# Prompt delta rule: the 16x16 diagonal blocks of the triangular inverse are solved on VectorE instead of four doubling levels on TensorE; the experts' low parts all on VectorE

## The reference

```
A = jnp.where(strict, jnp.einsum('nbhid,nbhjd->nbhij', kb, k) * decay, 0.0)
L = A + jnp.eye(C, dtype=A.dtype)
sol = lax.linalg.triangular_solve(L, rhs, left_side=True, lower=True, unit_diagonal=True)
```

## Time and profile before

| what | value |
|---|---|
| median of 3 runs | 3206.22 us (3206.04 to 3209.23) |
| the profiled execution | 3210.79 us, span 3209.2 us |
| PE busy | 2627.7 us (82%) |
| DVE busy | 1601.7 us (50%) |
| ACT, POOL busy | 1064.6 us (33%), 698.9 us (22%) |
| granted TensorE clock, mean | 0.903 of full |

### The profile page before, as it was taken

How to read it: one execution, slowest core, us unless ns; L and a number is a source line. 1 busy time by engine, 2 the same in 40 slices (tenths; PEclk the granted TensorE clock), 3 DMA queues, 4 the chain that set the end, 5 groups by cost and what they waited for, 6 DMA issues and landing times. The chain is left out here.

```text
span 3209.2 us, 36850 instructions
## 1 busy us (share of the span) xinstructions
PE 2627.7 (82%) x13079; PEld 1953.9 (61%) x13080; DVE 1601.7 (50%) x1864; ACT 1064.6 (33%) x1565; POOL 698.9 (22%) x559
## 2 busy tenths in 40 slices
PE   5799999999998666789987998969648888888840
PEld 2477777777777543644447998945336666666620
DVE  2245445444545321124444456423458888888815
ACT  3123323323332100023333423312136566656602
POOL 1033133123213020011221000000043343344212
PEclk8999999999999767589998999989779999999975
DMA  7300000000000123021106444552369999999625
GB/s 289 133 7 27 20 7 27 27 0 27 27 1 1 45 61 139 1 79 40 39 0 221 140 129 126 149 165 82 119 223 349 334 342 338 337 337 341 236 105 176
DMA packets 252401, 420.95 MB, mean 131 GB/s; under 512 B 30563, under 2 KB 202099, under 8 KB 224228
## 3 DMA queue, kind: packets, MB, share of 16 engines
q1 hardware_dynamic: 228172, 355.72, 32.6%
q0 software_dynamic: 11168, 39.12, 3.4%
q10 hardware_dynamic: 13000, 25.30, 2.1%
HBM read 375.48 MB, written 46.65 MB: 132 GB/s over the span
## 5 line engine op out<-in xcount | busy, mean ns | idle before, releaser
L2356 DVE TENSOR_TENSOR ex_w_r<-ex_w,ex_wh 128x2048 fp32r<-128x2048 f32 x160 | 457.3, 2875 | 110.6 <-ACT ex_wh L2297 110.6
L2297 ACT ACTIVATE ex_wh<-ex_w 128x2048 fp32r<-128x2048 f32 x192 | 360.2, 1912 | 236.8 <-DVE ex_y L2374 98.0
L777 PE MATMUL gd_ps<-hT,gd_w 128*128 128x352 f32 x768 | 245.5, 468 | 13.7 <-DMA gd_w<-in_w_in_dram 8.2
L1716 PE MATMUL mg_psum<-mg_xl,mg_wh 128*128 128x352 f32 x768 | 252.2, 328 | 0.0
L2221 POOL TENSOR_TENSOR ex_w_r<-ex_w,ex_wh 128x2048 fp32r<-128x2048 f32 x32 | 160.2, 5009 | 409.4 <-ACT ex_wh L2297 409.4
L777 PEld LDWEIGHTS gd_ps<-hT,gd_w 128*128 128x128 f32 x768 | 144.0, 195 | 87.0 <-DMA gd_w<-in_w_in_dram 10.0
L1776 DVE TENSOR_TENSOR mg_w_r<-mg_w,mg_wh 128x1024 fp32r<-128x1024 f32 x96 | 129.1, 1349 | 126.7 <-ACT mg_wh L1729 126.6
L542 POOL TENSOR_TENSOR gd_am<-gd_AT,levels 128x512 f32<-128x512 f32 x112 | 143.7, 1300 | 182.8 <-DVE gd_AT L710 96.5
L615 ACT ACTIVATE gd_T<-gd_x 128x512 f32<-128x512 f32 x96 | 57.3, 597 | 325.8 <-PE gd_x L797 325.8
L1729 ACT ACTIVATE mg_wh<-mg_w 128x1024 fp32r<-128x1024 f32 x96 | 101.4, 1056 | 189.5 <-DVE mg_out L1803 126.3
L1888 PE MATMUL op_mix<-op_w,op_mT 128*128 128x512 f32 x288 | 131.0, 615 | 25.5 <-DMA op_w<-in_w_out_dram 25.5
(11 more groups left out here) (571 smaller groups left out, 5689.0 us busy)
## 6 DMA issues: line engine op xcount, KB each, us to landing
ex_w<-in_w_gate_dram SPq DMA_DIRECT2D x64, 1024.0 KB, 7.6
ex_w<-in_w_up_dram SPq DMA_DIRECT2D x64, 1024.0 KB, 7.3
ex_w<-in_w_down_dram SPq DMA_DIRECT2D x64, 1024.0 KB, 6.4
ada_w<-in_w_ada_dram SPq DMA_DIRECT2D x24, 1024.0 KB, 14.5
mg_w<-in_w_in_dram SPq DMA_DIRECT2D x48, 512.0 KB, 3.7
gd_w<-in_w_in_dram SPq DMA_DIRECT2D x32, 512.0 KB, 4.5
expert_out_scratch<-ex_y ACTq DMA_DIRECT2D x32, 512.0 KB, 8.0
mg_w<-in_w_br_gdn_dram SPq DMA_DIRECT2D x24, 512.0 KB, 3.6
```

The lines of the kernel that those rows point to most:

```text
L777: last = nc.tensor.matmul(dst, w[t][:, n, :], c.hT[:, n, at], start=(n == 0), stop=(n == KD - 1))
L1716: last = nc.tensor.matmul(pm[b][q][:, 0:R], a, x, start=(m == 0 and v == 0), stop=(m == KD - 1 and v == 2))
L2297: nc.scalar.activation(wh[at][:], wl[b][u][:], ACT.Copy).then_inc(w_high, 1)
L2356: nc.vector.tensor_tensor(wl_r[b][u][:], wl[b][u][:], wh[at][:].bitcast(F32), ALU.subtract).then_inc(low_v, 1)
```

## The change

In `delta_prompt`, levels 0 to 3 go. In their place AT is stored to a scratch tensor in device memory, SP loads all 64 diagonal 16x16 blocks of the head's eight tiles, one block to a partition (`gd_Ab`, 64x256), and DVE inverts them by forward substitution: 15 columns, each a product (`gd_Tb`) and a subtraction in `gd_Yb`, each waiting for the one before. Y and its transpose go back to scratch tensors whose other entries were zeroed once at the start, and are loaded as full tiles into `gd_Y` and `gd_YT`. Levels 4 and 5 run as before; level 6 uses the 64-row halves of the tiles that are not zero. PE now does four projection units (8 halves) ahead of level 4, none inside level 4, and two units inside levels 5 and 6. V's SiLU on DVE stands behind the whole substitution, and PE's turn of v waits for it.

In `experts`, all six low parts are DVE's, ACT alone copies y (1024 columns), POOL keeps the gathers. w_down is loaded as rows k*128+p (`kmajor`), in pieces of 4 KB instead of 8 KB, and the hidden activation is written without a stride.

```diff
+                    for g in range(2):
+                        sp.wait_ge(ats, i * 8 + g * 4 + 4)
+                        sp.dma_start(image(c.at_s, g), v4(AT[g][:])).then_inc(at_out, 16)
+                    sp.wait_ge(at_out, i * 32 + 32)
+                    sp.dma_start(Ab[:], diagonal(c.at_s)).then_inc(blocks_in, 16)
+                    sp.wait_ge(solved, i + 1)
+                    sp.dma_start(diagonal(c.y_s), Yb[:]).then_inc(y_out, 16)
+                    sp.dma_start(diagonal(c.yt_s), YbT[:]).then_inc(y_out, 16)
+                    sp.wait_ge(y_out, i * 32 + 32)
+                    for g in range(2):
+                        sp.dma_start(v4(Y[g][:]), image(c.y_s, g)).then_inc(y_in[g], 16)
+                        sp.dma_start(v4(YT[g][:]), image(c.yt_s, g)).then_inc(y_in[g], 16)
...
+                    dve.wait_ge(y_out, i * 32)
+                    step(nc.vector.tensor_copy(Yb[:], Ib[:]), 0)
+                    dve.wait_ge(blocks_in, i * 16 + 16)
+                    for j in range(BS - 1):
+                        n, m = BS - 1 - j, j + 1
+                        tmp = Tb[:, 0:n * m].rearrange("p (a b) -> p a b", b=m)
+                        step(nc.vector.tensor_tensor(tmp, Ab[:, j, m:BS].unsqueeze(2).to_broadcast([64, n, m]), Yb[:, j:j + 1, 0:m].to_broadcast([64, n, m]), ALU.mult), 2 * j + 1)
+                        step(nc.vector.tensor_tensor(Yb[:, m:BS, 0:m], Yb[:, m:BS, 0:m], tmp, ALU.subtract), 2 * j + 2)
+                    step(nc.vector.tensor_copy(YbT[:], Yb[:].rearrange("p r q -> p q r")), STEPS - 1)
...
-                def low_last(e, b):
-                    pool.wait_ge(w_high, e * UNITS + 10 if not (isinstance(e, int) and e == NE - 1) else 6 * NE)
-                    nc.gpsimd.tensor_tensor(wl_r[b][5][:], wl[b][5][:], wh[down_slot(b, 1)][:].bitcast(F32), ALU.subtract).then_inc(low_p, 1)
...
-                    nc.scalar.activation(y[b][:, 0:512], pd[:, 0:512], ACT.Copy).then_inc(y_act, 1)
-                    act.wait_ge(y_act, e + 1)
-                    act.wait_ge(y_dve, e + 1)
+                    nc.scalar.activation(y[b][:], pd[:], ACT.Copy).then_inc(copied, 1)
+                    act.wait_ge(copied, e + 1)
...
+                    if not is_first(e):
+                        down_low(e + -1, 1 - b, 1)
```

More of the change, by code:

```diff
@@ L436, in delta_prompt @@
     C4 = 4 * P
+    BS = 16
+    NQ = P // BS
+    STEPS = 2 * BS
+    HP = P // 2
+    IMAGE = NQ * (BS * P + BS)
     C3 = TA // 3
@@ new lines, in body @@
+                    pe.wait_ge(v_silu, i + 1)
+                    pe.wait_ge(capped, i * 8 + 8)
+                    for g in range(2):
+                        turn(pp[g], y[2], g).then_inc(vturned, 1)
+                    if nxt:
+                        for half in range(2):
+                            project(1, 0, half, i + 1)
+                    for l in (4, 5, 6):
+                        for g in range(2):
+                            if l == 4:
+                                pe.wait_ge(kts, i * 2 + g + 1)
+                                pe.wait_ge(y_in[g], i * 32 + 32)
+                            else:
+                                pe.wait_ge(ys, i * 4 + (l - 5) * 2 + g + 1)
+                            if l < 6:
+                                pe.wait_ge(lvl, i * 4 + (l - 4) * 2 + g + 1)
+                                quad(X[g][0], am[g][l % 2], Y[g]).then_inc(p1, 1)
+                            else:
+                                for n in range(4):
+                                    lo, hi = slice(n * P, n * P + HP), slice(n * P + HP, (n + 1) * P)
+                                    last = nc.tensor.matmul(X[g][0][:, lo], AT[g][0:HP, n * P:(n + 1) * P], Y[g][0:HP, lo], start=True, stop=True)
+                                last.then_inc(p1, 1)
+                            if l == 5:
@@ L875, in body @@
                             else:
-                                quad(X[g][1], T1[g], YT[g]).then_inc(p3, 1)
-                        if nxt:
-                            project((l - 1) // 3, (l - 1) % 3, 1, i + 1)
+                                for n in range(4):
+                                    lo, hi = slice(n * P, n * P + HP), slice(n * P + HP, (n + 1) * P)
+                                    last = nc.tensor.matmul(X[g][1][:, hi], T1[g][HP:P, n * P:(n + 1) * P], YT[g][HP:P, hi], start=True, stop=True)
+                                last.then_inc(p3, 1)
+                        if nxt and l > 4:
+                            project(1, l - 4, 1, i + 1)
                     for g in range(2):
-                        pe.wait_ge(yts, i * 12 + 10 + g + 1)
+                        pe.wait_ge(yts, i * 6 + 4 + g + 1)
                         pe.wait_ge(k2s, i * 4 + g * 2 + 2)
@@ L2177, in before, with last_down @@
             return n if is_first(e) else e * UNITS + (n - 2)
+        def last_down(e, half):
+            return 6 * NE - 2 + half if isinstance(e, int) and e == NE - 1 else e * UNITS + (8 + half)
         def up_slot(e, b, u):
@@ L2251, in down @@
                 def down(e, b, half):
-                    if half:
-                        pe.wait_ge(low_p, e + 1)
-                    else:
-                        pe.wait_ge(low_v, e * (UNITS - 1) + 9 if not (isinstance(e, int) and e == NE - 1) else 5 * NE)
+                    pe.wait_ge(w_low, last_down(e, half) + 1)
                     h = wh[down_slot(b, half)]
@@ L2302, in down_high @@
                 def down_high(e, b, n, h):
-                    high(e, b, n, 4 + h, down_slot(b, h), e * UNITS + (8 + h) if not (isinstance(e, int) and e == NE - 1) else 6 * NE - 2 + h)
+                    high(e, b, n, 4 + h, down_slot(b, h), last_down(e, h))
                 def x_high(e):
@@ L2386, in body @@
                     else:
[L2387 removed]
+                        for h in range(2):
+                            down_low(e, b, h)
                     dve.wait_ge(twos, e + 1)
                     dve.wait_ge(used, before(e, 4))
[L2390 to L2391 removed]
+                    nc.vector.tensor_tensor(gu[:], two[:], pu[:], ALU.mult).then_inc(prods, 1)
                     if nxt:
@@ L2395, in body @@
                         up_low(e + 1, 1 - b, 2)
-                    if not is_first(e):
-                        out(e + -1, 1 - b, i, before(e, 6))
                 for u in range(3):
```

196 lines of the change are left out of this document (97 added, 99 removed).

## The result

The changed kernel takes 3020.11 us (median of 4 runs, 3019.03 to 3023.98), the kernel before beside it 3206.15 (3206.04 to 3209.23): a ratio of 0.942, 95% interval 0.9403 to 0.9436. The forecast was 3047 with a range of 2998 to 3120. So the sign and the range held, and 27 us of gain were missing from it; of its two causes, the one for the experts was named wrongly.

The account below looks back on a forecast made before the run. PE was taken to bound the prompt heads, a DVE chain with POOL's low part the experts. Gains of 73 + 86 = 159 from the profiled 3210.8 gave 3051.8, less 4.6 to the median, so 3047 us; range 2998 to 3120.

Parts of the forecast that it names:

- Heads, 11 us each: Prompt heads: each of seven gets 11 us shorter, 77 over seven; ends of 15 and 4 a head.
- the 1.5 booked behind level 6 for the low clock: End of a head: the clock may fall again in PE's gap; half of about 3 us added, 460.8 to 462.3.
- Stores of 64 B, 5.0 us: Heads, behind the substitution: two stores of 1024 pieces of 64 B take 5.0 us, between bounds of 2 and 8.4.
- the predicted idle 2.8 us before level 4: Heads: PE idles 2.8 us until Y of group 0 is loaded, and level 4 starts at 438.9.
- Level 6 saves 0.9: Heads: level 6 with half the columns saves 0.9 us, taken between nothing and 1.8.
- Last head 4 us worse: Last head, without projections: turn of k to w product goes from 41.6 to 44.8 us, taken as 4 worse.
- An expert at 18.8: Experts: PE becomes the bound at 18.8 us each, from 21.67, with 18.5 to 19.2 possible; 86 us over 30.
- So the experts are held by a chain over DVE: the low part that POOL works on: Experts before: POOL's 4.96 us low part stretches a DVE one from 2.28 to 5.35; PE idles 2.46 an expert.
- Rival 1: Experts: transfers bound them at 20.4 us each, so the gain is 38 and the time 3095; chance 0.17.
- Rivals 2 and 3: Heads: 64 B stores or substitution 6 us longer, 3099 us, chance 0.12; 64 B pieces landing like ab_w, 3343, 0.03.
- Rival 4: Experts: DVE's low parts stay stretched by POOL's gathers, an expert stays near 21.5 us, time 3127; chance 0.04.

Follow-up runs that it names:

- e8: Changed kernel with level 6 on whole tiles again (mask, four full matmuls a product, whole copies): 3025.86 us.
- e12: Changed kernel with only the low part of unit 5 in the experts given back to GpSimd; ACT still copies all of y: 3026.19 us.
- e5: Changed kernel with one of three products left out of gate and up, 56 matmuls an expert instead of 72: 2978.98 us.
- e6: Changed kernel with PE doing unit 0 of the next head's second projection before the turn of v instead of after: 3033.75 us.
- e7: Changed kernel with the substitution between second and third tap of v's convolution, and v turned behind level 4's first half: 3017.47 us.
- e11: Changed kernel with substitution between v's second and third tap, projection before v's turn, v's copies behind level 4's first T1, whole-tile level 6: 2998.53 us.
- e10: Changed kernel with SyncE writing the 64 solved blocks out a second time and waiting for that before loading Y and its transpose: 3054.11 us.

## Why the prediction came out as it did

- **Heads, 11 us each: right in the sum, in part by luck.** 11.6 us, 81 over seven. The wait for v's SiLU was 3.2 for 2.5 predicted, and the substitution with its copies 9.2 for 8.6. Behind that, errors cancelled. Level 4 starts 27.1 us after the turn of k, for 27.4 predicted, but because PE is still at the slow projection and not because Y lands then; level 4 is 0.6 shorter than predicted (3.8), level 6 is 1.7 longer (10.0), and the 1.5 booked behind level 6 for the low clock is not there but in the projection.
- **Stores of 64 B, 5.0 us: mis-sized.** A store lands in 2.5 us and the pair within 3.3 of the first issue (409.84 to the loads' issue at 413.12). I had taken a value between 2 and 8.4; the truth lies near the lower end. So the predicted idle 2.8 us before level 4 didn't come. The half clock took part of the gain back: the projection in the gap took 6.6 us instead of 4.9.
- **Level 6 saves 0.9: wrong sign.** It costs 0.8 (e8). My lower bound was "nothing", by the weight load; a loss was left out of the range.
- **Last head 4 us worse: wrong.** 80.4 before, 80.5 after, of which the part from the turn of k to the w product is 41.7 against 41.6. Of the 4, 0.8 was rounding up from 3.2. Level 4 starts 25.7 us after the turn of k instead of 27.3 (904.42 to 930.07 in the changed kernel; the stores), and levels 4 to 6 with the low clock take 16.0 instead of 17.5.
- **An expert at 18.8: mis-sized.** PE without waits needs 18.18 us (turns of x at 2709.67, 2727.85, 2746.03), below my lower end of 18.5: I had charged to the work what the pipe loses around each wait (my reading; no run takes the 1.0 us between 19.2 and 18.18 apart). The stage gained 99.5 instead of 86.
- **"So the experts are held by a chain over DVE: the low part that POOL works on": wrong.** This is the step that failed. The chain did run over VectorE, but its link was VectorE's half copy of y, for which ACT waited 6.2 us an expert with the next high part behind it. Once ACT copies y alone, both stretched instructions can stay and nothing is lost (e12). What is open is how much the stretch added to the wait while the copy was split: up to 3.06 us, since it stands ahead of that copy. The sum came out because PE's idle time before was counted right, whoever caused it, and because the edit also moved the copy, which I had booked only as more work for ACT; as to the cause, that is luck. From the profile I had read who was long; the page's own row of the high parts shows who was waited for.
- **Rival 1, transfers at 20.4 us: refuted.** 399 to 407 GB/s were carried in the loop and 420 in e5. The share of 0.94 was that of a queue that followed the engines. The figure of 358 GB/s (the Trainium skill, DMA: Bandwidth & Descriptors, Where 436 GB/s comes from) didn't bind here, with one core running: the measurement is above it. But the bound is near: 17.5 us an expert.
- **Rivals 2 and 3: refuted** by landings of 2.5 to 2.7 us for 1024 pieces of 64 B; the 23.8 us of ab_w stayed a case of its own (23.7 after), whose reason no run here tested. **Rival 4: refuted.** With the gathers still running, all 192 low parts take 2274 to 2294 ns.
- **The unbooked 11 us:** 9.4 + 4.0 - 2.3 come from the start, the middle and the rest behind, and lie within what these scatter from kernel to kernel (the middle by 13.6 us, the rest behind by 5.0 among the kernels in which ACT copies y).

## What to carry to other kernels

An instruction that grows longer is not yet a cause: ask which engine waits, for whom, and what is queued behind the wait. When a computing engine issues the store of a tile, as ACT does here, its program has to wait for every other writer of the tile, with all the work behind it (6.2 us an expert). Where two chains end within a microsecond of each other, filling the wait for one shows the other and can lose (e6: +10 us in the heads); shorten both, and put the gap where cheap work stands behind it, since the low clock fell on what came next (6.59 us for a projection in the changed kernel, 2.07 for eight records of level 4 in e6). For effects under 10 us on a kernel of 3000, compare stages by fixed marks of the profile, not totals.

## What the runs showed of the hardware

- A matmul with 64 contraction rows and 64 columns isn't shorter than one with 128 and 128: 1.10 us for eight records against 1.05.
- VectorE and GpSimd instructions with two inputs in SBUF slow each other: 128x2048 takes 2.28 us alone and 4.52 to 5.35 beside GpSimd's of the same size (4.96). Beside pieces of 128x512 the longest was 3.13, and each of GpSimd's pieces took 2.1 instead of 1.04. Small steps suffer too: in e7 the first steps of the substitution took 0.81 to 0.97 beside GpSimd instructions of 1.03, and 0.19 from the moment GpSimd was done, as if each had to sit one out. The Trainium skill (GPSIMD Engine Reference, Specifications) names this contention for VectorE instructions with two SBUF inputs or in a 2-port perf mode. The copy of 64x256, with one input, shows it too: 1.12 us in the middle of a GpSimd instruction and 0.28 where it fell between two (e7); which mode it ran in no trace shows.
- The granted clock fell to 0.50 after PE gaps of 3.2 us (after) and 4.3 us (e6), and to 0.56 and 0.59 in two windows of 2 us after three gaps of 0.6 to 1.1 us close together (e7); it stayed at 1.00 in e11 with gaps of 0.6, 0.2 and 1.2. The gap alone doesn't settle it: behind the same wait of 2.01 us ahead of the turn of k it fell to 0.50 in the changed kernel and in e7 (the projection took 6.44 and 6.59 us), and stayed at 1.00 in e10 (4.90).
- A stage with the same program took 1312.8 to 1326.4 us over 14 profiles. Its mean granted clock was 0.84 to 0.85 in all of them, so the mean clock doesn't tell them apart; the cause was not settled.
